# Hybrid decoder block on one core: index scores from fp32r halves, row sums of the x squares in 32-token pieces, and another ScalarE order at two places

## The reference, cut to what matters

```
h = rms_norm(x, norm1_g) * (1.0 + scale1) + shift1
proj = h @ w_in
(q_lat, a_k, a_v, k_idx, w_idx, b_q, b_f, b_i, b_g, gate_a, gate_b) = split_cols(proj, COL_SIZES)
q_lat = rms_norm(q_lat, q_lat_norm_g)
q_idx = (q_lat @ w_uq_idx).reshape(B, L, IDX_HEADS, IDX_DIM)
k_idx = rms_norm(k_idx, k_idx_norm_g)
...
rel = relu(einsum('bthd,bsd->bths', q_idx, k_idx))
score = einsum('bth,bths->bts', w_idx * idx_scale, rel)
top_val, top_idx = top_k(where(causal, score, -inf), topk)
...
y = square(relu(h2 @ w_mlp1 + b_mlp1)) @ w_mlp2 + b_mlp2
```

## Time and profile before

| what | value |
|---|---|
| median of 3 runs | 771.15 us (770.37 to 771.26) |
| the profiled execution's own time | 771.27 us |
| its span | 769.4 us |
| PE busy | 761.0 us (99% of the span) |
| DVE busy | 630.9 us (82%) |
| ACT busy | 364.7 us (47%) |
| POOL busy | 62.7 us (8%) |
| the chain that ended last | PE 94%, DVE 3%, ACT 2% |

### The profile page before, as it was taken

One profiled execution on the slowest core, in us unless ns is written; L12 is line 12 of the kernel. 1 busy time (PEld: TensorE's weight loads), 2 busy tenths in 40 slices (PEclk: granted clock), 3 DMA queues, 4 the chain that ended last, 5 costly groups with the idle time before them and its releaser, 6 DMA issues.

```text
span 769.4 us, 13224 instructions
## 1 busy us (share of the span) xinstructions
PE 761.0 (99%) x5208; PEld 645.8 (84%) x5208; DVE 630.9 (82%) x1129; ACT 364.7 (47%) x577; POOL 62.7 (8%) x64
## 2 busy tenths in 40 slices
PE   7999999999999999999999999999999999999998
PEld 6876878777878777778889988889999888889998
DVE  6975999778998677769966999879998766779996
ACT  5466524455344376654332555654333354454341
POOL 5015344200000000000012000000000000000000
PEclk9999999999999999999999999999999999999999
DMA  9943223221221233345556255312333433213331
GB/s 349 403 140 110 83 83 107 75 67 56 80 86 58 85 107 126 145 142 184 200 180 203 83 165 191 109 55 86 108 110 109 138 110 102 89 55 111 110 110 56
DMA packets 27643, 95.50 MB, mean 124 GB/s; under 512 B 3009, under 2 KB 3393, under 8 KB 27586
## 3 DMA queue, kind: packets, MB, share of 16 engines
q1 hardware_dynamic: 27296, 94.51, 36.8%
q10 hardware_dynamic: 290, 0.20, 0.1%
HBM read 92.61 MB, written 2.10 MB: 123 GB/s over the span
## 4 chain that ended last, share of the span: by engine, by line
PE 94%; DVE 3%; ACT 2%; issue 1%; DMA 1%; DVEq 0%; ACTq 0%
PE bank L1612 10%; PE bank L1614 10%; PE bank L1613 10%; PE bank L2187 7%; PE bank L2189 7%; PE bank L2188 7%; PE bank L1662 5%; PE bank L1841 2%; PE bank L1798 2%; PE bank L1842 2%; PE bank L1843 2%; PE bank L2015 2%; PE bank L1800 2%; PE bank L1799 2%; PE bank L2017 2%; PE bank L2016 2%
## 5 line engine op out<-in xcount | busy, mean ns | idle before, releaser
L1612 PE MATMUL bank<-h_hi,w_hi 128*128 128x512 f32 x328 | 128.2, 391 | 0.6 <-ACT relu_u L886 0.6
L1613 PE MATMUL bank<-h_lo,w_hi 128*128 128x512 f32 x328 | 127.7, 389 | 0.0
L1614 PE MATMUL bank<-h_hi,w_lo 128*128 128x512 f32 x328 | 127.6, 389 | 0.0
L526 ACT ACTIVATE w_hi<-w_raw 128x1024 fp32r<-128x1024 f32 (+2 forms) x94 | 97.4, 1039 | 30.7 <-PE bank L1819 9.4
L1087 DVE TENSOR_TENSOR w_lo<-w_raw,w_hi 128x1024 fp32r<-128x1024 f32 x68 | 83.5, 1236 | 11.7 <-ACT w_hi L526 11.7
L1612 PEld LDWEIGHTS bank<-h_hi,w_hi 128*128 128x128 f32 x328 | 61.6, 188 | 13.4 <-ACT relu_u L886 0.8
L2187 PE MATMUL bank<-u_hi,wf_hi 128*128 128x256 f32 x256 | 72.6, 284 | 0.1
L2189 PE MATMUL bank<-u_hi,wf_lo 128*128 128x256 f32 x256 | 72.4, 283 | 0.0
L2188 PE MATMUL bank<-u_lo,wf_hi 128*128 128x256 f32 x256 | 72.4, 283 | 0.0
L1614 PEld LDWEIGHTS bank<-h_hi,w_lo 128*128 128x128 f32 x328 | 61.6, 188 | 12.9
L1613 PEld LDWEIGHTS bank<-h_lo,w_hi 128*128 128x128 f32 x328 | 61.6, 188 | 12.6
(11 more groups left out here) (319 smaller groups left out, 1890.4 us busy)
## 6 DMA issues: line engine op xcount, KB each, us to landing
w_raw<-in_units SPq DMA_DIRECT2D x117, 512.0 KB, 3.3
ada_raw<-in_ada SPq DMA_DIRECT2D x16, 512.0 KB, 10.3
ada_even<-in_ada SPq DMA_DIRECT2D x16, 512.0 KB, 4.5
ada_odd<-in_ada SPq DMA_DIRECT2D x16, 512.0 KB, 4.4
w_raw<-in_units SPq DMA_DIRECT2D x8, 448.0 KB, 10.6
xT<-in_xt SPq DMA_DIRECT2D x4, 512.0 KB, 5.3
out<-xT SPq DMA_DIRECT2D x7, 256.0 KB, 2.5
w_raw<-in_units SPq DMA_DIRECT2D x1, 256.0 KB, 5.1
```

What stands on the lines that cost most here:

```text
L526: nc.scalar.activation(w_hi[:, s, 0:width], w_raw[:, s, 0:width], ACT.Copy).then_inc(hi_ready, 1)
L1612: mm(bank[b][:], w_hi[:, slot, j], rhs_hi(i), start=f, stop=False)
L1613: mm(bank[b][:], w_hi[:, slot, j], rhs_lo(i), start=False, stop=False)
L1614: end = mm(bank[b][:], w_lo[:, slot, j], rhs_hi(i), start=False, stop=l)
```

## The change

Five parts.

1. The squares of x: ACT squares slices 0, 1, 2, 3, 4 and 6, DVE 5 and 7; the additions of pairs go. PE makes `row_sums` of each slice (16 float32 matmuls of 32 columns by 1 moving column) into four columns of bank 7, with idle products of 128x128 between them (5 times 2, then 1), and 7 in the place of 5 after the spread. The load of ACT's table for the root stands before the last square and no longer after it.
2. The latents: ACT rounds both, copies and squares the index key, and only then squares the latents; DVE's `lat_lo` waits for the rounding alone. PE waits for the first latent's square before it writes into bank 0.
3. The index queries and keys are split: `qi_hi` is ACT's copy (in fp32r), `qi_lo` two subtractions on DVE, `ki_hi` a copy on ACT and `ki_lo` a subtraction on DVE. These three kinds of instructions are new, and the scores wait for `qi_lo`, `ki_lo` and the head weights.
4. `scores` makes three fp32r matmuls per head in the place of one float32 matmul, the two heads of a pair in turns. It waits for the relu of both heads of the pair that last stood in the banks.
5. The first MLP units: in the first half `up_relu` of unit 2 stands before `tforms_hi` of the pair 0, its square behind it.

```diff
-            x_square(6)
-            x_square(7)
             nc.scalar.activation(warm[:, 2:4], ident[:, 2:4], ACT.Sqrt)
-            act.wait_ge(xsq_summed, KC // 2)
-            nc.scalar.activation(XRS, bank[7][:, 0:T:P], ACT.Sqrt, scale=1.0 / D, bias=EPSC
+            x_square(6)
+            act.wait_ge(xsq_summed, 1)
+            nc.scalar.activation(XRS, bank[7][:, 0:TB], ACT.Sqrt, scale=1.0 / D, bias=EPSC
...
                 nc.scalar.activation(lat_hi[:, k], bank[k][:], ACT.Identity,
-                                     scale=col[:, V_QG + k:V_QG + k + 1])
-                nc.scalar.activation(sq[:, k], bank[k][:], ACT.Square).then_inc(latsq_ready, 1)
+                                     scale=col[:, V_QG + k:V_QG + k + 1]).then_inc(lathi_ready, 1)
...
             nc.scalar.activation(kw_sq[0:HD, :], bank[2][0:HD, :], ACT.Square).then_inc(kwsq_ready, 1)
+            for k in range(RC):
+                act.wait_ge(lat_ready, k + 1)
+                nc.scalar.activation(sq[:, k], bank[k][:], ACT.Square).then_inc(latsq_ready, 1)
...
-                nc.scalar.activation(qiT[:, m], bank[SCORE_BANK[m]][:], ACT.Copy).then_inc(qi_taken, 1)
+                nc.scalar.activation(qi_hi[:, m], bank[SCORE_BANK[m]][:], ACT.Copy).then_inc(qi_taken, 1)
...
+            act.wait_ge(ki_ready, 2)
+            nc.scalar.activation(ki_hi[:], kiT[:], ACT.Copy).then_inc(kihi_ready, 1)
...
                     up_relu(h, j)
+                    if h == 0 and j == 2:
+                        tforms_hi(0, 0)
                     up_square(h, j)
...
-                    if j % 2 and j < MH - 3:
+                    if j % 2 and j < MH - 3 and (h or j > 1):
                         tforms_hi(h, j // 2)
...
-            x_add(0)
             c_product(0)
-            x_add(1)
             c_product(1)
-            dve.wait_ge(x_loaded[2], 16)
-            step(v.tensor_tensor(x_sq[:, 5], xT[:, 5], xT[:, 5], ALU.mult))
-            x_add(2)
-            x_add(3)
+            for k in X_DVE:
+                x_square(k)
...
+            dve.wait_ge(ada_used, 2 * KC)
+            for m in range(RC):
+                dve.wait_ge(qi_taken, m + 1)
+                v.tensor_tensor(qi_lo[:, m], bank[SCORE_BANK[m]][:], qi_hi[:, m].bitcast(F32),
+                                ALU.subtract).then_inc(qilo_ready, 1)
             dve.wait_ge(lat_root, 1)
             v.scalar_tensor_tensor(out=LEPS, in0=LRS, scalar=EPS, in1=LRS, op0=ALU.mult, op1=ALU.mult)
...
+            dve.wait_ge(kihi_ready, 1)
+            v.tensor_tensor(ki_lo[:], kiT[:], ki_hi[:].bitcast(F32), ALU.subtract).then_inc(kilo_ready, 1)
...
-            for p in range(KC // 2):
-                pe.wait_ge(xsq_added, p + 1)
-                for b in range(TB):
-                    t = slice(b * P, (b + 1) * P)
-                    end = mm(bank[7][:, t], x_sq[:, 2 * p, t], ones[:], start=p == 0 and b == 0,
-                             stop=p == KC // 2 - 1 and b == TB - 1)
-                end.then_inc(xsq_summed, 1)
+            for s, k in enumerate(X_ACT[:5]):
+                pe.wait_ge(xsq_ready, s + 1)
+                row_sums(7, 0, x_sq[:, k], P, s == 0, False)
+                idle_products(2)
+            pe.wait_ge(xsq_made, 1)
+            row_sums(7, 0, x_sq[:, X_DVE[0]], P, False, False)
+            idle_products(1)
+            pe.wait_ge(xsq_made, 2)
+            row_sums(7, 0, x_sq[:, X_DVE[1]], P, False, False)
+            pe.wait_ge(xsq_ready, len(X_ACT))
+            row_sums(7, 0, x_sq[:, X_ACT[5]], P, False, True).then_inc(xsq_summed, 1)
             idle_products(3)
             pe.wait_ge(xroot_ready, 2)
             row_spread(7, XRS).then_inc(xspread, 1)
-            idle_products(5)
+            idle_products(7)
...
-                for h in range(IH):
-                    r = HD * (h % 2)
+                q = slice(qb * P, (qb + 1) * P)
+                for g in range(IH // 2):
                     s = nscore[0]
-                    nscore[0] += 1
+                    nscore[0] += 2
                     if s >= IH:
-                        pe.wait_ge(rel_ready, s - IH + 1)
-                    mm(bank[SCORE_BANK[h]][:, 0:n], qiT[r:r + HD, h // 2, qb * P:(qb + 1) * P], kiT[r:r + HD, 0:n],
-                       start=True, stop=True).then_inc(score_done, 1)
+                        pe.wait_ge(rel_ready, s - IH + 2)
+                    for x, (qi, ki) in enumerate(((qi_hi, ki_hi), (qi_lo, ki_hi), (qi_hi, ki_lo))):
+                        for e in range(2):
+                            r = slice(HD * e, HD * (e + 1))
+                            end = mm(bank[SCORE_BANK[2 * g + e]][:, 0:n], qi[r, g, q], ki[r, 0:n],
+                                     start=x == 0, stop=x == 2)
```

More of the change, by code:

```diff
@@ L119, in hybrid_block @@
         kiT = place("kiT", RL + 12 * KB, [P, T])
-        qiT = place("qiT", RL + 16 * KB, [P, RC, T])
+        ki_lo = place("ki_lo", RL + 12 * KB, [P, T], F32R)
+        ki_hi = place("ki_hi", RB + 4 * KB, [P, T], F32R)
+        qi_hi = place("qi_hi", RL + 16 * KB, [P, RC, T], F32R)
+        qi_lo = place("qi_lo", RB, [P, RC, T], F32R)
         sq = place("sq", RL + 20 * KB, [P, 2, T])
@@ L214, in hybrid_block @@
         lb_ready, gqk_ready = sem("lb_ready"), sem("gqk_ready")
-        xsq_ready, xsq_added, xsq_summed, xroot_ready, xspread = (
-            sem("xsq_ready"), sem("xsq_added"), sem("xsq_summed"), sem("xroot_ready"), sem("xspread"))
+        xsq_ready, xsq_made, xsq_summed, xroot_ready, xspread = (
+            sem("xsq_ready"), sem("xsq_made"), sem("xsq_summed"), sem("xroot_ready"), sem("xspread"))
         a1_ready, xn_ready, hfull_ready = sem("a1_ready"), sem("xn_ready"), sem("hfull_ready")
@@ L219, in hybrid_block @@
         lat_ready, latsq_ready, latsq_added = sem("lat_ready"), sem("latsq_ready"), sem("latsq_added")
+        lathi_ready = sem("lathi_ready")
         kw_ready, kwsq_ready, k_taken = sem("kw_ready"), sem("kwsq_ready"), sem("k_taken")
+        kihi_ready, kilo_ready, qilo_ready = sem("kihi_ready"), sem("kilo_ready"), sem("qilo_ready")
         ki_summed, ki_root, ki_spread, ki_ready = (sem("ki_summed"), sem("ki_root"), sem("ki_spread"),
@@ L298, in ada_home @@
             return (ada_odd if i % 2 else ada_even), i % 2, i // 2
+        X_ACT, X_DVE = (0, 1, 2, 3, 4, 6), (5, 7)
         LOGIT_BANK = [[6, 4, 2, 3], [6, 7, 4, 5]]
@@ L546, in _ @@
             x_square(4)
+            nc.scalar.activation(warm[:, 2:4], ident[:, 2:4], ACT.Sqrt)
             x_square(6)
-            x_square(7)
-            nc.scalar.activation(warm[:, 2:4], ident[:, 2:4], ACT.Sqrt)
-            act.wait_ge(xsq_summed, KC // 2)
-            nc.scalar.activation(XRS, bank[7][:, 0:T:P], ACT.Sqrt, scale=1.0 / D, bias=EPSC
+            act.wait_ge(xsq_summed, 1)
+            nc.scalar.activation(XRS, bank[7][:, 0:TB], ACT.Sqrt, scale=1.0 / D, bias=EPSC
                                  ).then_inc(xroot_ready, 1)
@@ L999, in _, with x_square @@
             v.tensor_tensor(GQK, col[:, V_HQ:V_HQ + 1], col[:, V_HK:V_HK + 1], ALU.mult).then_inc(gqk_ready, 1)
-            def x_add(p):
-                dve.wait_ge(xsq_ready, [2, 4, 5, 7][p])
-                v.tensor_tensor(x_sq[:, 2 * p], x_sq[:, 2 * p], x_sq[:, 2 * p + 1], ALU.add).then_inc(xsq_added, 1)
+            def x_square(k):
+                dve.wait_ge(x_loaded[k // 2], 16)
+                v.tensor_tensor(x_sq[:, k], xT[:, k], xT[:, k], ALU.mult).then_inc(xsq_made, 1)
             def c_product(j):
@@ L1063, in _ @@
             for k in range(RC):
-                dve.wait_ge(latsq_ready, k + 1)
+                dve.wait_ge(lathi_ready, k + 1)
                 v.scalar_tensor_tensor(out=lat_lo[:, k], in0=bank[k][:], scalar=col[:, V_QG + k:V_QG + k + 1],
@@ L1068, in _ @@
             dve.wait_ge(t_lo, KC)
+            dve.wait_ge(latsq_ready, RC)
             v.tensor_tensor(lat_sq[:], sq[:, 0], sq[:, 1], ALU.add).then_inc(latsq_added, 1)
@@ L1691, in _ @@
                 b = SCORE_BANK[m]
+                if b < RC:
+                    pe.wait_ge(latsq_ready, b + 1)
                 for i, j in enumerate((m, 2 + m)):
@@ L1724, in scores @@
                 n = (qb + 1) * P
-                for h in range(IH):
-                    r = HD * (h % 2)
+                q = slice(qb * P, (qb + 1) * P)
+                for g in range(IH // 2):
                     s = nscore[0]
-                    nscore[0] += 1
+                    nscore[0] += 2
                     if s >= IH:
-                        pe.wait_ge(rel_ready, s - IH + 1)
-                    mm(bank[SCORE_BANK[h]][:, 0:n], qiT[r:r + HD, h // 2, qb * P:(qb + 1) * P], kiT[r:r + HD, 0:n],
-                       start=True, stop=True).then_inc(score_done, 1)
+                        pe.wait_ge(rel_ready, s - IH + 2)
[4 more added lines that the diff above has]
+                                     start=x == 0, stop=x == 2)
+                            if x == 2:
+                                end.then_inc(score_done, 1)
```

(4 more changed lines are left out.)

## The result

The changed kernel takes 775.25 us (median of 5 runs, 774.43 to 776.91) against 771.13 us before (median of 5): ratio 1.0058, 95% interval 1.0044 to 1.0072. It is slower, by 4.1 us; I had forecast 770.3 us. The profiled execution is the one of 775.25 us, with a span of 773.4.

A forecast was written before the change was run, and what follows sets the result against it. PE was taken as the bound, busy 99% of the span. From 771.27, MLP -0.7, scores -0.56, latents 0 and the start +0.25 gave 770.3 us; range 768.7 to 772.8.

The forecast's parts named there:

- MLP: First MLP units: unit 2's relu fits in ACT's idle time, so unit 4 starts earlier; -0.7 us, at worst 0.
- Scores: Score blocks: fp32r pairs run side by side; second block ends 0.20 us earlier, last gains 0.36; together -0.56 us.
- Halves: Split index queries and keys: ready at 65.2, scores begin at 65.73; nothing on the path, 0.5 us to spare.
- Latents: Index key's earlier square: PE's 0.65 us earlier start becomes a wait at the spread of KRS; 0 us.
- The start: Small sums with idle products replace 16 sums at the low clock; sums end at 13.4 against 13.15, +0.25 us.
- if the clock rises at about 12 as before: During the sums at the start: three sets and one idle product then follow at the high level, 1.34 us.
- the path from the root to 16.56 is unchanged: From ACT's root to the first slice at the start: no change in time, as no one else holds the sums.
- The sizes at the low level: Rounds at the start: a set 0.36 us (at most 0.72), two idle products 0.82, a round 1.18.
- a clock that rises later: Rival at the start: clock low to the sums' end, first slice at 19.0 to 20.1; 772.9 us, chance 0.19.
- less work in a microsecond: Ground for the late-clock rival at the start: small sums stream one column each, so PE does less work than before.

The follow-up runs named there:

- Experiment 9: Changed kernel with the old start or one set last, ACT's root KRS moved directly behind the moved squares: 769.33 us with the old start, 768.27 us with the other.
- old_start_krs: Changed kernel with the start as before, root KRS directly behind the moved squares and `ki_lo` before LEPS: 769.33 us, ratio 0.9977.
- hybrid_start: Changed kernel; start: one idle product, 12 full sums, one set of 16 small sums; root KRS earlier, `ki_lo` before LEPS: 768.32 us, ratio 0.9963.
- idle_first: Changed kernel with 14 idle products in one piece before the first set and none between the sets: 777.75 us, ratio 1.0087.
- full_sums: Changed kernel with each set of 16 sums of 32 columns replaced by 4 sums of 128 columns, one moving column: 782.62 us, ratio 1.0150.
- wide_idle: Changed kernel with each of the first five pairs of 128-column idle products replaced by one of 512 columns: 776.44 us, ratio 1.0067.
- no_idle_between: Changed kernel without the 11 idle products between the small sums; the 3 and 7 behind them stay: 772.63 us, ratio 1.0021.
- experiment 3: Changed kernel with its 32-column small sums replaced by whole-array sums of 128 columns, one moving column: 782.62 us, ratio 1.0150.
- experiment 7: Changed kernel with a start of one idle product, 12 full sums and one last set of 16 small sums: 768.32 us with KRS moved, 768.66 without.
- old_start: Changed kernel with squares, sums, idle products and ACT's order at the start as before, parts 2 to 5 kept: 769.56 us, ratio 0.9980.
- mlp_only: Kernel before, with part 5 alone (relu of unit 2 before the roundings of pair 0): 770.41 us, ratio 0.9985.
- the hybrid: Changed kernel with a start of one idle product, 12 full sums, one set of 16 small sums; three kernels: 768.32, 768.66 and 768.27 us.

## Why the prediction was wrong

- **MLP, right.** Forecast -0.7; trace -0.72, alone -0.8.
- **Scores, nearly right.** Forecast -0.56, trace -0.42. The first block takes 0.90 us (forecast 0.92) and the third 1.59 (1.56). The second should have ended 0.20 earlier; it ended 0.09 earlier. Its relu hangs, by the chain of waits, on ACT's weight split (1.06 us from 71.05) and the weighing of 2.24, not on the first block.
- **Halves, right.** 0.5 us to spare forecast, 0.54 found (70.40 to 70.94). LEPS was held for 2.09 us, as I had it: it ends at 69.51, POOL's second split at 64.73 + 4.76 = 69.49.
- **Latents, right.** The earlier start became a wait of PE at the spread of KRS, 0.46 us in the trace (forecast about 0.6), and the spread follows the first slice at 42.15 us as before. Experiment 9 shows what PE waited for: ACT's weight split and copies of the keys, which stood before the root.
- **The start, wrong.** Forecast +0.25, measured +5.27. The step that failed is "if the clock rises at about 12 as before". I carried the time of the rise over from a stretch of nothing but 128-column products to one in which 0.54 of every 1.69 us go to one-column sums. The clock rose at 21.7 and not at 12. So the root came 3.66 us later, and "the path from the root to 16.56 is unchanged" failed with it: at the low level that path took 5.00 us and not 3.39, which adds 1.61. The "about 12" was also the reading of a single execution: `old_start_krs` has the same start, and there the 32 records of the full sums took 5.53 us in place of 6.51, the high level came at about 9.5 and the first slice at 15.55.

```profile
6.61 5.53 PE L1670 MATMUL bank<-ones,x_sq 128*128 128x128 f32 x32 [0.52 <-DVE x_sq L1015]
```

What the runs show of the rise, side by side:

| kernel | what PE ran | high level from |
|---|---|---|
| before | full products from 6.6 | about 12.2 |
| old_start_krs | full products from 6.6 | about 9.5 |
| hybrid_start | full products from 6.0 | about 10.3 |
| idle_first | full products from 6.0 | about 12.1 |
| changed | sets and pairs from 6.0, full from 16.7 | about 21.7 |
| full_sums | one-column sums and pairs from 6.1, full from 24.5 | not before 29.6 |
| wide_idle | sets and 512 columns from 6.0 | about 18.4 |
| no_idle_between | sets from 6.2, a stop of 3.06, full from 14.4 | about 18.4 |

As long as sets, or one-column sums of the whole array, came between 128-column pairs, the level stayed low; a change of the form was not needed for that (experiment 3). All rows fit one reading: one-column sums between the full products held the rise back. In wide_idle, with 512 columns between the sets, the rise came at 18.4 all the same. What it is in the one-column sums that does so, no run separates.

- **The sizes at the low level.** I took 0.36 us for a set, a row at the high clock: it was 0.54 at the low one, and 0.36 in experiment 7 at the high one. A pair of idle products between sets took 1.15 and not 0.82. So a round was 1.69 and not 1.18.
- **The rival "a clock that rises later"** was the case, and I gave it 0.19. Its own price was too small: I let the sums end at 13.6 to 16.4, but took the first slice from 13.6 and 14.7. With the upper end, 16.4 + 5.4 = 21.8, it would have had the first slice and the time right (771.27 - 1.26 + 21.8 - 16.56 = 775.25 us), but by luck: sets of 0.72 us were too dear (0.54) and idle products of 0.41 between them too cheap (1.15 a pair), and the sums ended at 16.76. Against it I had nothing but the row of the kernel before; "less work in a microsecond" spoke for it, and I had written that down.

## What to carry to other kernels

If a term of a sum depends on TensorE's clock, price it at both levels and carry both ends through to the last step, and don't take the time of the rise from a stretch in which the engine did other work, nor from one execution. Small matmuls are cheap once the clock is up: put the full products first and the small ones last (experiment 7: 0.36 us a set, where the changed kernel paid 0.54 and its clock stayed low). Replacing few large instructions by many small ones also costs instructions: look in the DMA view for packets of the instruction queue while loads fill the queues.

## What the runs showed of the hardware that I had not expected

- PE stopped for 3.06 and 4.86 us after exactly 223 matmul records, with one instruction packet in each stop and the DMA queues full. That it stood for want of instructions and that the packet ended the stop is inferred: the packets begin at 11.0 to 11.25 and at 16.25 to 16.5, each some 2.5 us before PE goes on (13.74 and 18.72). No run moved them.
- A sum over the whole array with one moving column takes (12.95 - 11.38) / 4 = 0.39 us at the low level (experiment 3), about as much as an idle product of 128 columns (0.41 in the earlier trace rows).
- The time of the rise differs between executions of the same start. The 32 records of the full sums took 6.51 us in the kernel before, 6.04 and 6.33 in `old_start` and `mlp_only`, and 5.53 in `old_start_krs`, all with that start; the 24 of the hybrid's took 4.65, 4.18 and 5.42 in its three kernels. The Trainium skill (TensorE: Matmul & The Clock Gate, "What's actually happening") says that the number of matmuls before the rise varies between runs of one kernel; these rows agree. A difference of a microsecond between two profiles at the start is therefore no finding by itself.
